# The last stage of a two-block transformer kernel: the low part of A's columns goes from VectorE to GpSimd, and seven more tiles of V are split into high and low

## The reference, cut to what matters

```python
q = (x @ w_q).reshape(B, S, PEER_HEADS, 2, PEER_HALF)
...
ids = jnp.take_along_axis(cand_i, pos, axis=-1)
g = jax.nn.softmax(best_s, axis=-1).astype(x.dtype)
...
u = jnp.take(expert_u, it, axis=0)
act = jax.nn.gelu(jnp.einsum('td,tkd->tk', xt, u)) * gt
v = jnp.take(expert_v, it, axis=0)
return jnp.einsum('tk,tkd->td', act, v)
```

## Time and profile before

| | |
|---|---|
| median of 3 runs | 3305.74 us (3304.07 to 3306.32) |
| the profiled execution's own time | 3306.93 us |
| its span | 3304.9 us |
| busy: PE, DVE, ACT, POOL | 2896.9 (88%), 2588.3 (78%), 1714.5 (52%), 624.2 (19%) |
| last stage, DVE's first aside to its last Al | 2929.87 to 3291.30 us |
| PE's granted clock in it | 1.00 |

### The profile page before, as it was taken

The page is one execution under the profiler, slowest core; times in us unless marked ns, Lnnn a source line. Parts: engine busy times, 40 slices in busy tenths (PEclk is TensorE's granted clock), DMA queues, the critical chain, the costliest instruction groups (busy, mean ns, idle before and its releaser), DMA issues.

```text
span 3304.9 us, 37651 instructions
## 1 busy us (share of the span) xinstructions
PE 2896.9 (88%) x14041; PEld 2376.6 (72%) x14041; DVE 2588.3 (78%) x3916; ACT 1714.5 (52%) x2802; POOL 624.2 (19%) x533
## 2 busy tenths in 40 slices
PE   8999999999999999999999999997655441279998
PEld 7998998888888888888888888872222241157776
DVE  7786767776456878787556676689998899999998
ACT  6554555664444555555445674222434589645444
POOL 0000000000000000000000000375545333346664
PEclk9999999999999999999999999999887555589999
DMA  7555555555555555555556557999999999989998
GB/s 238 160 150 159 163 164 167 180 168 199 191 178 189 182 191 191 188 192 200 192 185 235 160 172 242 335 413 411 410 421 413 419 427 418 416 325 391 394 391 315
DMA packets 424909, 870.12 MB, mean 263 GB/s; under 512 B 18615, under 2 KB 248920, under 8 KB 391192
## 3 DMA queue, kind: packets, MB, share of 16 engines
q1 hardware_dynamic: 347776, 454.20, 41.1%
q0 software_dynamic: 75936, 413.17, 30.8%
q10 hardware_dynamic: 1016, 0.35, 0.0%
HBM read 865.56 MB, written 2.10 MB: 263 GB/s over the span
## 4 chain that ended last, share of the span: by engine, by line
PE 72%; DVE 12%; DMA 8%; issue 4%; ACT 2%; POOL 2%; DVEq 0%; SPq 0%; ACTq 0%; POOLq 0%
PE W L1792 15%; PE W L1843 12%; PE W L1845 12%; PE W L1844 12%; PE W L1789 8%; PE W L2010 5%; DMA Ub<-in_peer_u,ids 5%; DVE Ub L3197 5%; DVE X L3255 2%; PE T L2006 2%; DMA Vx<-in_peer_v,vid 2%; PE M L1896 2%; PE W L1747 1%; DMA Vr<-in_peer_v 1%; POOL Ub L3348 1%
## 5 line engine op out<-in xcount | busy, mean ns | idle before, releaser
L2746 DVE TENSOR_TENSOR wl<-raw,wh 128x1024 fp32r<-128x1024 f32 (+1 forms) x720 | 850.6, 1186 | 557.8 <-ACT wh L2150 556.1
L2150 ACT ACTIVATE wh<-raw 128x1024 fp32r<-128x1024 f32 (+1 forms) x720 | 740.7, 1031 | 887.3 <-PE W L1845 571.9
L1792 PE MATMUL W<-u,wh 128*128 128x512 f32 x2176 | 674.9, 396 | 1.3 <-DVE cw L2662 0.7
L3197 DVE CUSTOM_DVE_ANT_0 Ub<-Ub,W 128x2048 f32<-128x2048 f32 x226 | 511.8, 2283 | 27.3 <-DMA Ub<-in_peer_u,ids 19.5
L1789 PEld LDWEIGHTS W<-u,wl 128*128 128x128 f32 x2176 | 396.5, 188 | 87.6 <-issue 0.7
L1843 PE MATMUL W<-wh,u 128*128 128x512 f32 (+1 forms) x1152 | 436.4, 379 | 1.2 <-DVE u L3106 1.0
L1845 PE MATMUL W<-wh,u 128*128 128x512 f32 (+1 forms) x1152 | 428.2, 372 | 0.0
L1844 PE MATMUL W<-wl,u 128*128 128x512 f32 (+1 forms) x1152 | 427.7, 371 | 0.0
L1789 PE MATMUL W<-u,wl 128*128 128x256 f32 x2176 | 422.1, 280 | 0.3 <-DVE u L2708 0.3
L1982 PE MATMUL M<-Vx,diag 128*128 128x512 f32 x416 | 217.3, 674 | 144.2 <-DMA Vx<-in_peer_v,vid 88.5
L1792 PEld LDWEIGHTS W<-u,wh 128*128 128x128 f32 x2176 | 336.4, 189 | 7.0 <-DVE wl L2746 0.9
(11 more groups left out here) (405 smaller groups left out, 4587.4 us busy)
## 6 DMA issues: line engine op xcount, KB each, us to landing
raw<-in_w_in SPq DMA_DIRECT2D x128, 1024.0 KB, 5.1
raw<-in_w_up SPq DMA_DIRECT2D x88, 1024.0 KB, 4.8
Vr<-in_peer_v SPq DMA_DIRECT2D x128, 512.0 KB, 6.4
raw<-in_w_down SPq DMA_DIRECT2D x44, 1024.0 KB, 5.0
raw<-in_w_in SPq DMA_DIRECT2D x144, 256.0 KB, 3.4
raw<-in_w_out SPq DMA_DIRECT2D x32, 1024.0 KB, 5.0
raw<-in_w_proj_a SPq DMA_DIRECT2D x16, 1024.0 KB, 5.0
Wb<-in_peer_w_q SPq DMA_DIRECT2D x16, 1024.0 KB, 7.8
```

What stands on the lines that cost most here:

```text
L1792: return q.matmul(pr[h][:, :], H[:, k, col(h)], u[:, k0 + k, :, :].rearrange("p a t -> p (a t)"), start=first, stop=last)
L2150: q.activation(wh[:, s % NS, 0:b.half], r, ACT.Copy).then_inc(s_hi, 1)
L2746: q.tensor_tensor(wl[:, s % NS, 0:b.half], r, wh[:, s % NS, 0:b.half].bitcast(F32), SUB).then_inc(s_lo, 1)
L3197: q.tensor_tensor_reduce(U[:, :], U[:, :], inputs[:, :], 1.0, 0.0, MUL, ADD, dots[t][:, k:k + 1]).then_inc(s_dot, 1)
```

## The change

`RAW` goes from 16 to 128: only tile 0 is whole, and the tiles 16, 32, 48, 64, 80, 96 and 112 are split like the others. `low_a` moves from DVE's function to GpSimd's, with the same waits and the same operands. So that it can stand between the asks, the planner adds only the first five asks in `make`, and in `dense` one ask behind each aside, for the row five later.

```diff
-RAW = 16
+RAW = 128
...
-        for i in range(ASIDES):
+        for i in range(NA):
             self.add("get_aside", i)
...
             while a < min(ASIDES, max(3, j * ASIDES // 125)):
                 self.add("aside", a)
+                if a + NA < ASIDES:
+                    self.add("get_aside", a + NA)
                 a += 1
             self.add("low", j)
             self.add("column", j)
             self.add("low_a", j)
             self.add("mul", j)
...
 def vector(...)
-            def low_a(j):
-                if whole_tile(j):
-                    return
-                both = strided(AA[:, 4 * j:4 * j + 1], [(A1_o - A0_o) // 4, 2], [4 * P, 32], [1, 4])
-                e.wait_ge(s_ah, j + 2)
-                q.tensor_tensor(Al[j % 2][:, :, :].rearrange("p t (g x) -> p t g x", x=4), both,
-                                Ah[j % 2][:, :, :].bitcast(F32).rearrange("p t (g x) -> p t g x", x=4), SUB).then_inc(s_al, 1)
...
 def gpsimd(q)
+            def low_a(j):
...
```

More of the change, by code:

```diff
@@ L3297, in vector @@
                   "a_gate": a_gate, "a_lo": a_lo, "turn_hi": turn_hi, "peer": peer, "xn": xn_part, "top_sides": top_sides, "top_pairs": top_pairs,
-                  "top_ids": top_ids, "top_weights": top_weights, "dot": dot, "weigh": weigh, "spike": spike, "low": low_v, "low_a": low_a,
+                  "top_ids": top_ids, "top_weights": top_weights, "dot": dot, "weigh": weigh, "spike": spike, "low": low_v,
                   "rows": rows, "aside": aside, "upper_scale": upper_scale, "close": close})
@@ L3372, in get_aside @@
                 q.indirect_dma_start(side_b[i % NA][:, :], None, ev_half, bass.IndirectOffsetOnAxis(index, 0)).then_inc(s_place[LANDS["aside", i][0]], 16)
+            def low_a(j):
+                if whole_tile(j):
+                    return
+                both = strided(AA[:, 4 * j:4 * j + 1], [(A1_o - A0_o) // 4, 2], [4 * P, 32], [1, 4])
+                e.wait_ge(s_ah, j + 2)
+                q.tensor_tensor(Al[j % 2][:, :, :].rearrange("p t (g x) -> p t g x", x=4), both,
+                                Ah[j % 2][:, :, :].bitcast(F32).rearrange("p t (g x) -> p t g x", x=4), SUB).then_inc(s_al, 1)
             walk({"setup": setup, "reload": reload, "load_gf": load_gf, "loads": loads,
-                  "peer_loads": peer_loads, "get_u": get_u, "get_v": get_v, "get_aside": get_aside})
+                  "peer_loads": peer_loads, "get_u": get_u, "get_v": get_v, "get_aside": get_aside, "low_a": low_a})
         block = ctx.enter_context(nc.Block())
```

## The result

The changed kernel takes 3343.93 us (median of 4; 3335.41 to 3345.52) against 3306.03 (4 runs of the kernel before). The ratio is 1.0107, 95% interval 1.0095 to 1.0119: slower by 38 us. The prediction was 3356 with a range of 3312 to 3400, so the sign and the main mechanism are borne out, and the forecast is 12 us above what was measured; two of its terms were off, in opposite directions.

What follows compares the result with a forecast made beforehand. PE, DVE and DMA were within 3% of their limits, with DVE alone to set the pace after the change. On DVE -40.8 + 7.9 + 90.2 - 8.8 + 2.0 = +50.5 us on 3305.7: about 3356, range 3312 to 3400.

Steps and rivals of the forecast that it cites:

- Rival B: Last stage: no contention worth the name, PE is the bound, -9.4 us or 3296; chance 0.12.
- Terms 1 and 2: Last stage: Al leaves DVE, -40.8 us; seven tiles become split, +7.9 on DVE, -5.0 on PE off the path.
- Term 3: Last stage: Al on GpSimd shuts DVE out 0.71 us a tile, 127 times, +90.2 us.
- Term 4: Last stage: DVE's waits for ACT are filled once DVE alone sets the pace, -8.8 us.
- rival A: Last stage: GpSimd waits, DVE is not held up, GpSimd is the bound; halfway +12 us, 3318; chance 0.12.
- Term 5: Start of last stage: three asks ahead of the first Al and a GpSimd library reload, together +2.0 us on DVE.
- The signs: Last stage: DVE records stretched or gaps of 0.6 to 0.8 us, PE near 85% busy, DMA share below 1.

Runs made afterwards that it cites:

- The zero fill with the good order: Changed kernel with Al replaced by two zero fills, asks behind their tile's Al, Al 1, 2 and 3 each ahead of the first asks: 3298.82 us.
- the zero fill: Changed kernel with GpSimd's subtraction for Al replaced by two zero fills that read nothing: 3314.71 us, ratio 1.0022.
- the PSUM input: Changed kernel with Vl's second input taken from PSUM instead of Vh: 3330.18 us, ratio 1.0074.
- the doubled Al's run: Changed kernel with Al computed twice on GpSimd, one after the other: 3479.04 us, ratio 1.0524.
- The order experiment: Changed kernel with GpSimd's asks of a tile behind that tile's Al instead of ahead of it: 3333.24 us, ratio 1.0076.
- The copy: Changed kernel with GpSimd's subtraction for Al replaced by a copy of A's columns, half the reading: 3321.47 us, ratio 1.005.

## Why the prediction was right, and where its terms were off

**What bounds it.** Three resources within 3% of their limit, as the prediction had it. The zero fill with the good order shows the distance to the next limit: 7.5 us for a DVE relieved of all of Al. Rival B, no contention, was put at 3296; the kernel that comes nearest to its condition measured 3298.8. The real Al does not meet that condition.

**Terms 1 and 2** (-40.8 and +7.9 on DVE, PE's 5.0 off the path) stand as far as the sum below shows; no run measures them by themselves. The split alone measured 1.0005.

**Term 3, right in kind, and half as large again as measured.** "I take it that this holds both ways": the stretched Vl, the zero fill (1224 ns) and the PSUM input (1215 ns) show it from three sides. The size: Vl is 1543 - 1218 = 325 ns longer, 127 times, 41.3 us; additions 1402 - 1278 = 124 ns, 128 times, and little on the rest, 17 us. Together 58 us, 0.46 for each Al, where 0.71 and +90.2 were predicted. Two things were mis-sized. GpSimd's record is 0.73 us undisturbed, nearer the upper bound of 0.74 than the 0.63 taken, yet DVE is held only for 1.76 - 1.22 = 0.54 of it. In the timeline above Al has 0.61 us left when the addition ends, and the Vl behind it has begun 0.07 before that: 0.54. So the hole is the part of Al behind the addition's end less the overlap of DVE's records, where the prediction took the whole of Al and put the overlap on top. And not each Al costs so much, 0.46 on average: an Al that falls in a pause of DVE, as the one of 0.72 us at 3202.84 in the doubled Al's run does, holds nothing up.

**Term 4, wrong.** The 8.8 us that DVE waited for ACT were to be filled, -8.8. They rose to 21.2, +12.4 (13.1 in the second profile, +4.3). The prediction saw one bound, DVE, and let GpSimd's queue "fit, barely". In the middle of the stage that was right: DVE waits 0.8 us from 3040 to 3249, and the tiles of 4.05 us there are its own second additions. At the edges it was not. 6.1 us of the waits stand at the start, where PE got its first Al late, 6.8 from 2995 to 3037, behind PE's wait of 2.13 us for an Al and the slower clock that followed, and 7.4 from 3249 on, in the rhythm of 2.83 and 3.70. There PE waits for Al, ACT's Vh waits for PE and DVE for Vh. So rival A, GpSimd late and DVE waiting for it, was not another case but a part of this one. The order experiment, which leaves the stretch at 58 us and the waits at 8.7, puts that part at about 11 us. What two asks in a row ahead of an Al cost is not priced, since no run here with the real Al spreads them.

The sum by the measured terms is -40.8 + 7.9 + 58 + 12.4 = 37.5 us, against 38.7 between the two spans. The same sum for the asks behind Al, with 58 of stretch and 8.7 + 1.4 of waits (1.4 for rows), is -40.8 + 7.9 + 58 + 1.3 = 26.4, against 27.5 between the medians. In the changed kernel's second profile Vl average 1588 ns and additions 1389, 62 us of stretch, DVE waits 13.1 us for Vh, and the sum is 33.4 against 37.1 between the spans, with 2.6 us of it a later start than in the first. So the stretch is steady at 58 to 62 us, and the waits differ by 8 from one execution to the next. The predicted +50.5 came out only 12 us high since one error of -32 on term 3 and one of +21 on term 4 met in part. That the total was better than its parts is luck.

**Term 5** is not confirmed in size. The first split product came 2.7 us later in the first profile of the changed kernel (2938.26 against 2935.55) and 5.3 later in the second (2940.83), but it also moves between kernels that leave the start alone (2933.32 with the split alone). The reload costs nothing that can be seen:

```profile
L3373 POOLq MODIFY_POOL_CONFIG  x2: 38/40/43, 2937.2 to 2937.2; - x2
```

Two instructions of 38 and 43 ns at 2937.2, and the first Al starts at 2937.3. The 1.3 us taken were too much, no wait of several us stands ahead of the first Al, and the Trainium skill's 6 us for a freshly loaded kernel (GPSIMD Engine Reference, "Instruction dispatch") does not show here. What came in its stead is in the last section.

**The signs.** Vl and additions stretched in the records and the DMA share below 1, as said; DVE's part of the stage took some 398 us where 412 were forecast and 361.4 measured before. GpSimd is busy for 91% of 2950 to 3250 us, which the prediction had as a sign of rival A, but with DVE idle, and DVE is not. PE was busy for 94%, not 85. PE's steps from tile to tile show where its loss lies, as what they take above 2.72 us: 13 us in 80 ordinary tiles of mostly 2.87, 27 in the 18 longest, nearly all with two additions or the slower clock of the last section, and 10 in eleven of 3.5 to 3.7, most of them in the last 30. Before, it was 10 us in all, and 5 for the whole tiles.

## What to carry to other kernels

Before work goes to GpSimd because it "waits", ask whether it would read SBUF while DVE runs instructions with two SBUF inputs: here 0.34 us saved on DVE came back as 0.46, and the asks' own lengths (0.94 beside PSUM inputs, 1.65 beside SBUF ones) had told so beforehand. Look also at what a producer on a queue has in front of it, at the start of a stage above all: in the zero fill, the first Al ahead of the asks brought PE's first product forward by 4.8 us. Where several engines are within 3% of their limits, add up the two largest queues, not one, and ask of a long tile whether the engine that sets the pace has a gap in it. Here it had none: the 1.2 us were a second addition on DVE, though PE's wait was put down to GpSimd.

## What the runs showed of the hardware that was not expected

PE's granted clock fell three times in the changed kernel's last stage, for 3.4 us each, and each time behind a wait of PE. The busy time by stretch of the changed kernel:

```profile
2930.00:2938.00 8.00, 4.55 (x21) 2.36 (x19) 7.79 (x8) 5.38 (x9) 5.67 (x4) 1.00 0.58 176
2938.00:2943.00 5.00, 4.74 (x14) 3.82 (x15) 1.20 (x1) 0.16 (x1) 1.78 (x2) 0.66 0.64 246
...
2982.00:2988.00 6.00, 4.33 (x19) 3.01 (x17) 5.90 (x6) 2.73 (x4) 5.51 (x5) 1.00 1.00 390
2988.00:2994.00 6.00, 5.55 (x17) 4.45 (x18) 4.19 (x3) 0.92 (x2) 5.13 (x5) 0.72 0.87 322
```

Its PE at the first and the second of them:

```profile
2938.26 1.19 PE L2012 MATMUL W<-Vh,Ah 128*128 128x512 f32 x2 [3.49 <-POOL Al L3373]
2939.25 1.05 PE L2012 MATMUL W<-Vl,Ah 128*128 128x512 f32 x2
...
2942.18 0.62 PE L2012 MATMUL W<-Vh,Al 128*128 128x512 f32 x2
...
2988.45 0.70 PE L2012 MATMUL W<-Vh,Ah 128*128 128x512 f32 x2 [2.13 <-POOL Al L3373]
...
2990.36 1.05 PE L2012 MATMUL W<-Vh,Ah 128*128 128x512 f32 x2
```

PE had stood 3.49 us at the first and 2.13 us at the second, then ran at 1.2 GHz instead of 2.4: the tile took 4.38 and 4.41 us where 2.72 is the rule. The tile behind such a wait costs 1.7 us more. But it does not come behind each: in the second profile of the same kernel the clock fell once in the stage, at the start, and a wait of 1.95 us was followed by full speed:

```profile
2940.00:2945.00 5.00, 4.17 (x12) 3.37 (x13) 1.77 (x2) 0.00 (x0) 2.35 (x2) 0.66 0.70 267
2990.00:2996.00 6.00, 6.00 (x26) 4.55 (x26) 5.14 (x5) 3.92 (x5) 5.65 (x5) 1.00 1.00 395
3016.00:3021.00 5.00, 4.92 (x21) 3.90 (x22) 5.00 (x4) 1.37 (x2) 4.73 (x4) 1.00 0.89 315
```

```profile
3016.08 0.70 PE L2012 MATMUL W<-Vh,Ah 128*128 128x512 f32 x2 [1.95 <-POOL Al L3373]
```

That execution took 3343.83 us, as long as the others, so the three falls can't be counted as 5 of the 38 us. Before, PE waited 1.02 us at the start of the stage and kept its clock, and with Al 1 ahead of the asks (the zero fill in the good order) the second tile came 2.82 us after the first.

The price of a short GpSimd instruction for DVE is not its record's length. The subtraction held DVE 0.54 us where the two met, out of 0.73 or more, and 0.46 on average. The copy, 0.40 us undisturbed, held it 0.09 on average and 0.30 at most (the longest Vl, 1506 ns). The fill held it for no time that shows.
